# Attention's queries and keys kept channel by token, rotated from the bank by VectorE and GpSimd

## The chip, the cores and the metric

The kernel runs on 1 core of a Trainium2 chip. The metric is the device time of one execution in microseconds (us), the lower the better. The engines are TensorE (PE in the profile, its weight loads PEld), VectorE (DVE), ScalarE (ACT), GpSimd (POOL) and SyncE (SP), which here only starts DMAs. Each runs its own instructions in order, and they meet through semaphores.

## The reference, cut to what matters

One layer, 512 tokens, width 1024, all in float32. The normed input is multiplied by one wide matrix whose columns are split into sixteen parts; two branches follow (a sparse attention that takes the 128 best keys by an index score, and an mLSTM), then a gated merge.

```python
h = rmsnorm(x, norm_g[l])
(a_q, a_k, a_v, a_z, i_q, i_k, i_w,
 b_q, b_k, b_v, b_z, b_o, b_i, b_f, g_a, g_b) = jnp.split(h @ w_in[l], offsets, axis=-1)
q_a = partial_rope(a_q.reshape(Bsz, S, A_HEADS, A_HEAD_DIM), pos)   # 8 heads of 64
k_a = partial_rope(a_k.reshape(Bsz, S, A_HEADS, A_HEAD_DIM), pos)

def partial_rope(x, pos):            # of each 64 channels the first 16 turn
    ...
    x1, x2, rest = x32[..., :half], x32[..., half:rd], x32[..., rd:]
    out = jnp.concatenate([x1 * cos - x2 * sin, x1 * sin + x2 * cos, rest], axis=-1)
```

The attention's logits need `q_a` and `k_a` with channels on the partitions, the other way round than a product with tokens on the partitions leaves them.

## The kernel before

**Units and quarters.** A product of float32 numbers is made as three matmuls of rounded parts: `w_hi` and `w_lo` are a weight and its remainder, `h_hi` and `h_lo` those of the normed input (`three`, lines 1486 to 1488). The input projection is cut into units, each one PSUM bank `pj` of 128 by 512, made of 24 matmuls. `GROUPS` orders them: `iq0`, `iq1`, `aq`, `ak`, `bq`, `bk`, `bv`, `av`, `bo`, `bz`, `az`; a group is four units (three for the two `iq`). Units are written `bq0` to `bq3` below. In `aq` and `ak` a unit is one tile of 128 tokens, all 512 channels (token by channel). In `CHAN_GROUPS` (`bq`, `bk`) a unit is 128 channels, all 512 tokens.

A unit has four quarters, and `plan()` hangs every other job on a quarter, by number: `ak` is quarters 44 to 59, `bq` 60 to 75, `bk` 76 to 91, `bv` 92 to 107, `av` begins at 108. All engines walk the same table in the same order, so the table sets what is queued behind what. At a unit's last quarter ScalarE first empties the bank (`evacuate`, which also feeds VectorE), then does that quarter's side jobs, then rounds weights (`round_slot`, line 875), then the silu of the unit before (line 1043). GpSimd makes each weight's remainder (`remainder`, line 529). VectorE's own work of a unit (`unit(u)`) comes behind all side jobs of its quarters.

**What unit u + 2 waits for.** There are two `pj` banks, so TensorE may start a unit only when the unit two before has been read (`wait_unit_read`):

```python
elif UNITS[u] in STAGED:
    eng.wait_ge(rotated, STAGED.index(UNITS[u]) + 1)
elif UNITS[u][0] in CHAN_GROUPS:
    eng.wait_ge(conv_done, u - UNIT[("bq", 0)] + 1)
```

For `bq` and `bk` that is `conv(b)` on VectorE: three multiply-adds of about 510 elements from the bank (line 1234), after ScalarE's start of it (`conv_acc`, line 1000).

**Queries and keys of the attention before.** A unit of `aq` or `ak` is copied by ScalarE into `stage` (line 992); VectorE turns the 16 rotated channels of each head from the bank (three operations, lines 1138, 1140, 1141); TensorE turns the tile over with four transposes into a bank `tr` (line 1541); ScalarE copies it into `q_a` (line 904), or for keys rounds it into `k_parts` (line 913, two halves of 64 partitions), and VectorE writes the remainders, again from the bank (line 1259, two). This `stage_chan` job stands six quarters behind the unit's first.

**VectorE's other work here.** `round_plan` hangs the rounds of the top-k search on quarters: a round is a maximum (line 1223) and a replacement (line 1224). From quarter 73 on two rounds, of the second and of the first score tile, stand together every three quarters.

Of the kernel before, what the change touches and what calls it, by code (L numbers as in the profile page):

```python
# [19 lines left out]
ALU = mybir.AluOpType  # L20
# [18 lines left out]
ROT = A_DIM // 4  # L39
HALF = ROT // 2  # L40
# [20 lines left out]
CHAN_GROUPS = ("bq", "bk")  # L61

# [4 lines left out]
STAGED = [u for u in UNITS if u[0] in ("iq0", "iq1", "aq", "ak")]  # L67
# [44 lines left out]
def plan():  # L112
# [10 lines left out]
    put(first["iq0"] + 8, "gate_rows", 1)  # L123
    put(first["iq0"] + 8, "gate_rows", 0)
    put(first["iq1"] + 3, "gate_cols")
    for n, u in enumerate(STAGED):
        put(4 * UNIT[u] + 4 + 2, "stage_chan", n)

# [42 lines left out]
NOT_PE = ("scales_in", "scales", "decay_b")  # L171
# [52 lines left out]
def hybrid_kernel(nc, x, norm_g, w_in, conv_w, conv_b, b_igate, b_fgate, head_norm_g,  # L224
                  w_branch_a, w_branch_b, w_out, final_norm_g, ident_d, rope_d, out):
    ctx = ExitStack()
    with ctx:
# [58 lines left out]
        gate_l = const("gate_l", [P, TILES, 2 * B_HEADS])  # L286
# [45 lines left out]
        a_row = at("a_row", [B_HEADS, SEQ], F32, z_c + 8192)  # L332
        nm_row = at("nm_row", [B_HEADS, SEQ], F32, z_c + 10240)
# [207 lines left out]
        def wait_read(eng, job):  # L541
# [36 lines left out]
        def wait_unit_read(eng, u):  # L578
# [33 lines left out]
        def part(job, e):  # L612
# [4 lines left out]
            if g == "ak":  # L617
                cols = slice(j * P, (j + 1) * P)
                return src, k_parts[same, e, :, cols], k_parts[other, e, :, cols]
# [4 lines left out]
        def part_unit(job):  # L624

            return job[1] if job[1] < N_IQ else job[1] - TILES
# [22 lines left out]
        def _(sp):  # L649
# [36 lines left out]
            for n in range(LATE0):  # L686
# [48 lines left out]
        def _(pool):  # L735
# [13 lines left out]
            pool.memset(mask0[0:CHUNK, CHUNK:P], MASKED).then_inc(pool_step, 1)  # L749

            def side(p):
# [17 lines left out]
                for job in SIDE.get(p, []):  # L769
                    if job[0] == "decay_b":  # L770
# [74 lines left out]
        def _(act):  # L845
# [41 lines left out]
            def job_side(job):  # L887
# [13 lines left out]
                elif kind == "stage_chan" and STAGED[job[1]][0] == "aq":  # L901
                    j = STAGED[job[1]][1]
                    wait_full(act, job)
                    act.activation(q_a[:, j, :, :],
                                   bank_of(job)[:, :].rearrange("p (b t) -> p b t", t=P), ACT.Copy)\
                        .then_inc(q_a_turned, 1)
                elif kind == "stage_chan":
                    if STAGED[job[1]] == ("ak", 0):
                        act.wait_ge(gate_tok_made, 1)
# [46 lines left out]
                elif kind == "pv_b":  # L956
                    h, g = job[1:]
                    wait_full(act, job)
                    act.activation(cell[:, 2 * g:2 * g + 2, h, :],
# [20 lines left out]
            def evacuate(u):  # L980
# [6 lines left out]
                elif g in ("iq0", "iq1", "aq", "ak"):  # L987
# [18 lines left out]
                elif g == "av":  # L1006
                    act.activation(v_a[:, j, :], src[:, :], ACT.Copy).then_inc(done, 1)
# [8 lines left out]
            def split_queries(i):  # L1016
# [5 lines left out]
                act.wait_ge(q_a_turned, i + 1)  # L1022
# [88 lines left out]
        def _(dve):  # L1111
# [40 lines left out]

            def small(job):
# [597 lines left out]
```

## Time and profile before

| what | value |
|---|---|
| median of 3 runs | 505.25 us (505.06 to 505.51) |
| the profiled execution | 505.35 us, of which the span of its instructions 503.6 us |
| mean granted TensorE clock | 0.998 |
| TensorE busy | 494.5 us, 98% of the span |
| VectorE, ScalarE, GpSimd busy | 261.4, 239.2 and 213.0 us |

An engine's busy time is the union of its instructions. TensorE's matmuls overlap one another, so the pace of a stretch is read from the distance of starts, not from a row's duration. The averages hide stages: VectorE is busy in 52% of the span, but in 40 equal slices its digits read 9, 9, 9 from about 138 to 176 us, which is the stage of `bq`, `bk` and the first of `bv`.

### The profile page before, as it was taken

To read this page: it belongs to the slowest core of one execution; us is meant where nothing else is said; L and a number is where in the kernel's file an instruction comes from. 1 tells how busy PE (TensorE), PEld (TensorE's weight loads), DVE (VectorE), ACT (ScalarE), POOL (GpSimd) and SP (SyncE) were. 2 spreads that over 40 slices of the span, in tenths; PEclk is the share of its full clock that TensorE was granted. 3 is DMA by queue.
4 is the path that set the end of the run, shared out by engine and by line. 5 is a ranking of instruction groups with operands and counts; after the bars stand their busy time and mean duration, and the time that the engine had idled before them with its cause. 6 is when DMAs were issued, how large, how long until landed. Compare 5 with 4: busy or idle time off the path is not lost.

```text
span 503.6 us, 6823 instructions
## 1 busy us (share of the span) xinstructions
PE 494.5 (98%) x2518; PEld 411.6 (82%) x2518; DVE 261.4 (52%) x575; ACT 239.2 (47%) x434; POOL 213.0 (42%) x130
## 2 busy tenths in 40 slices
PE   8999999999999999999999999999999999999995
PEld 7688888888888888888788888888888888887885
DVE  3865777877899936525655567531111011125433
ACT  6757655555554455536568652413330333152322
POOL 0675131333344444247487451246534663373000
PEclk9999999999999999999999999999999999999999
DMA  8654432212343243112223112043234426453111
GB/s 284 188 153 128 126 87 79 84 48 80 83 111 99 85 117 104 52 43 85 57 70 85 43 43 65 20 125 104 62 87 125 126 58 193 126 149 144 42 55 72
DMA packets 44841, 48.94 MB, mean 97 GB/s; under 512 B 4996, under 2 KB 30212, under 8 KB 44808
## 3 DMA queue, kind: packets, MB, share of 16 engines
q1 hardware_dynamic: 43944, 47.65, 32.3%
q10 hardware_dynamic: 864, 0.86, 0.5%
q8 instruction: 20, 0.33, 0.3%
q14 instruction: 13, 0.11, 0.1%
HBM read 46.40 MB, written 2.11 MB: 96 GB/s over the span
## 4 chain that ended last, share of the span: by engine, by line
PE 94%; DMA 2%; SPq 1%; POOL 1%; ACT 1%; DVE 1%; issue 1%; DVEq 0%
PE pj L1486 24%; PE pj L1487 24%; PE pj L1488 24%; DMA w_raw<-in_w_in 2%; PE ob L1617 2%; PE tr L1606 2%; PE qb L1554 2%; PE qb L1553 2%; PE ob L1487 1%; PE qb L1487 1%; PE ob L1488 1%; PE qb L1488 1%; PE ob L1486 1%; PE qb L1486 1%; PE tr L1541 1%; PE qb L1601 1%
## 5 line engine op out<-in xcount | busy, mean ns | idle before, releaser
L529 POOL TENSOR_TENSOR w_lo<-w_raw,w_hi 128x1024 fp32r<-128x1024 f32 x70 | 168.9, 2424 | 156.3 <-ACT w_hi L875 156.0
L1486 PE MATMUL pj<-w_hi,h_hi 128*128 128x512 f32 x272 | 109.6, 403 | 0.0
L1488 PE MATMUL pj<-w_hi,h_lo 128*128 128x512 f32 x272 | 106.5, 392 | 0.0
L1487 PE MATMUL pj<-w_lo,h_hi 128*128 128x512 f32 x272 | 106.4, 391 | 0.0
L1486 PE MATMUL pj<-h_hi,w_hi 128*128 128x512 f32 (+1 forms) x200 | 78.1, 390 | 1.0 <-DVE h_lo L1129 1.0
L875 ACT ACTIVATE w_hi<-w_raw 128x1024 fp32r<-128x1024 f32 (+1 forms) x72 | 73.5, 1045 | 9.8 <-DMA w_raw<-in_w_out 6.3
L1488 PE MATMUL pj<-h_hi,w_lo 128*128 128x512 f32 (+1 forms) x200 | 77.9, 389 | 0.0
L1487 PE MATMUL pj<-h_lo,w_hi 128*128 128x512 f32 (+1 forms) x200 | 77.8, 389 | 0.0
L1488 PEld LDWEIGHTS pj<-w_hi,h_lo 128*128 128x128 f32 x272 | 51.1, 188 | 11.4
L1486 PEld LDWEIGHTS pj<-w_hi,h_hi 128*128 128x128 f32 x272 | 51.2, 188 | 8.3 <-issue 0.2
L1487 PEld LDWEIGHTS pj<-w_lo,h_hi 128*128 128x128 f32 x272 | 51.3, 188 | 8.0
L1443 DVE TENSOR_TENSOR prod<-qb,sig 128x512 f32<-128x512 f32 x8 | 5.5, 690 | 77.2 <-PE qb L1488 77.2
L1486 PEld LDWEIGHTS pj<-h_hi,w_hi 128*128 128x128 f32 (+1 forms) x200 | 37.3, 186 | 9.4 <-issue 1.3
L1488 PEld LDWEIGHTS pj<-h_hi,w_lo 128*128 128x128 f32 (+1 forms) x200 | 37.3, 186 | 8.1
L1487 PEld LDWEIGHTS pj<-h_lo,w_hi 128*128 128x128 f32 (+1 forms) x200 | 37.3, 186 | 7.8
L840 POOL TENSOR_TENSOR m_lo<-prod,m_hi 128x512 fp32r<-128x512 f32 x8 | 10.6, 1330 | 60.5 <-ACT m_hi L1088 60.5
L1211 DVE SCALAR_TENSOR_TENSOR score<-ob,idx_w,score 128x512 f32<-128x512 f32 (+2 forms) x45 | 27.7, 616 | 11.5 <-ACT ob L921 8.8
L921 ACT ACTIVATE ob<-qb 128x512 f32<-128x512 f32 (+2 forms) x48 | 22.0, 476 | 16.7 <-PE qb L1554 11.7
L966 ACT ACTIVATE probs<-probs,neg_max 128x128 f32<-128x128 f32 (+3 forms) x32 | 18.0, 562 | 23.3 <-DVE neg_max L1306 23.1
L1088 ACT ACTIVATE m_hi<-prod 128x512 fp32r<-128x512 f32 x8 | 5.1, 632 | 47.3 <-DVE prod L1446 47.3
L1315 DVE COPY probs_t<-tr 128x128 f32<-128x128 f32 (+3 forms) x32 | 15.6, 489 | 22.6 <-PE tr L1606 22.6
L1223 DVE MAX8 top<-score 128x8 f32<-128x512 f32 (+2 forms) x48 | 26.7, 556 | 0.9
(216 smaller groups left out, 817.3 us busy)
## 6 DMA issues: line engine op xcount, KB each, us to landing
w_raw<-in_w_in SPq DMA_DIRECT2D x60, 512.0 KB, 3.6
w_raw<-in_w_out SPq DMA_DIRECT2D x5, 512.0 KB, 3.5
x_tok<-in_x SPq DMA_DIRECT2D x4, 512.0 KB, 5.3
w_raw<-in_w_branch_a SPq DMA_DIRECT2D x8, 256.0 KB, 2.9
w_raw<-in_w_branch_b SPq DMA_DIRECT2D x8, 256.0 KB, 3.3
x_again<-in_x SPq DMA_DIRECT2D x1, 2048.0 KB, 9.3
w_late<-in_w_out SPq DMA_DIRECT2D x3, 512.0 KB, 6.1
out<-y_norm SPq DMA_DIRECT2D x4, 320.0 KB, 2.3
```

Source lines behind the costliest of these rows:

```text
L529: eng.tensor_tensor(lo[:, 0:m], raw_slot(n)[:, 0:m], hi[:, 0:m].bitcast(F32), ALU.subtract).then_inc(lo_by_dve if n in DVE_SLOTS else lo_b ...
L840: pool.tensor_tensor(m_lo[:, c, :], prod[:, c % 2, 0, :], m_hi[:, c, :].bitcast(F32), ALU.subtract)\
L875: act.activation(split_slot(n)[0][:, 0:m], raw_slot(n)[:, 0:m], ACT.Copy).then_inc(hi_made, 1)
L921: act.activation(ob[s % RELUS][:, 0:w], bank_of(job)[:, 0:w], ACT.Relu, scale=float(IDX_DIM) ** -0.5).then_inc(relu_made, 1)
L966: act.activation(probs[:, s % 2, 0:w], probs[:, s % 2, 0:w], ACT.Exp, scale=-1.0, bias=neg_max[:, s:s + 1], accum_out=p_sum[:, s:s + 1])\
L1211: ins = dve.scalar_tensor_tensor(out=acc, in0=ob[s % RELUS][:, 0:w], scalar=wt, in1=acc, op0=ALU.mult, op1=ALU.add)
L1223: link(dve.max(top8[:, i, :], acc))
L1315: dve.tensor_copy(probs_t[:, s % QUAD, 0:w], bank_of(job)[:, 0:w]).then_inc(probs_t_made, 1)
L1486: pe.matmul(bank, a_hi, b_hi, start=first, stop=False)
L1487: pe.matmul(bank, a_hi, b_lo, start=False, stop=False)
L1488: return pe.matmul(bank, a_lo, b_hi, start=False, stop=last)
L1553: pe.matmul(bank[:, 0:w], queries, ik_hi[:, 0:w], start=True, stop=False)
```

## The change

Units of `aq` and `ak` become channel by token: the weight is the stationary operand, and the bank holds 128 channels (two heads) by 512 tokens. ScalarE keeps the raw bank in `raw_chan`; VectorE multiplies the whole bank by a cosine table `cos_t` (ones where nothing turns) into `q_a` or `k_chan`. Four DMAs a group, started by ScalarE (`swap`), fetch the partner channels into `swapped`; GpSimd multiplies them by `sin_t` and adds them (`turn`, two operations for each of eight units). The `stage_chan` jobs of the two groups, with their transposes, go. For keys a new job `parts` follows each turn: ScalarE copies the turned keys into a `tr` bank and rounds them into `k_parts`, and VectorE writes the two remainders from that bank. The tables `cos_t` and `sin_t` come out of the transpose that the gates already had: `gate_rows` is now one job of four 128 by 128 transposes (was eight of 4 rows), `gate_cols` four (was eight); four ScalarE copies spread the tables, and five GpSimd memsets at the start blank the tiles.

```diff
+TURNED = ("aq", "ak")
+TURNS = [(g, b) for g in TURNED for b in range(KW)]
-STAGED = [u for u in UNITS if u[0] in ("iq0", "iq1", "aq", "ak")]
+STAGED = [u for u in UNITS if u[0] in ("iq0", "iq1")]
...
+    for k in range(4):
+        put(first["ak"] + k, "swap", k)
+        put(first["ak"] + 9 + 3 * 6 + k, "swap", KW + k)
+    for m in range(len(TURNS)):
+        p = first["ak"] + 6 + 6 * m
+        put(p, "turn", m)
+        if TURNS[m][0] == "ak":
+            put(p + 4, "parts", m - KW)
...
+                    if job[0] == "turn":
+                        m = job[1]
+                        g, b = TURNS[m]
+                        pool.wait_ge(rope_made, 4)
+                        pool.wait_ge(swap_in, 64 * (TURNED.index(g) + 1))
+                        pool.tensor_tensor(swapped[:, b, :], swapped[:, b, :], sin_t[:, :], ALU.mult).then_inc(sin_made, 1)
+                        pool.wait_ge(sin_made, m + 1)
+                        pool.wait_ge(cos_made, m + 1)
+                        part = swapped[:, b, :].rearrange("p (t n) -> p t n", n=P)
+                        pool.tensor_tensor(turned_rows(g, b), turned_rows(g, b), part, ALU.add).then_inc(turned, 1)
...
+                elif kind == "swap":
+
+                    n, k = divmod(job[1], 4)
+                    act.wait_ge(unit_out, UNIT[(TURNED[n], KW - 1)] + 1)
+                    if n:
+                        act.wait_ge(turned, KW * n)
+                    e, half = divmod(k, 2)
+                    to, src = A_DIM * e + HALF * half, A_DIM * e + HALF * (1 - half)
+                    act.dma_start(swapped[to:to + HALF, :, :], raw_chan[n][src:src + HALF, :, :]).then_inc(swap_in, 16)
+                elif kind == "parts":
+                    b = job[1]
+                    if b == 0:
+                        act.wait_ge(gate_tok_made, 1)
+                    act.wait_ge(turned, KW + b + 1)
...
+                    act.activation(tr[b % 2][:, :], k_chan[:, b, :], ACT.Copy).then_inc(k_in_bank, 1)
+                    for e in range(2):
+                        _, src, hi, _ = k_part(b, e)
+                        act.activation(hi, src, ACT.Copy).then_inc(k_hi_made, 1)
...
+                elif kind == "parts":
+                    b = job[1]
+                    for e in range(2):
+                        src, _, hi, lo = k_part(b, e)
+                        dve.wait_ge(k_in_bank, b + 1)
+                        dve.wait_ge(k_hi_made, 2 * b + e + 1)
+                        dve.tensor_tensor(lo, src, hi.bitcast(F32), ALU.subtract).then_inc(k_lo_made, 1)
...
+                if g in TURNED:
+                    if g == "ak" and j == 0:
+                        dve.wait_ge(swap_in, 64)
+                    if (g, j) == ("aq", 0):
+                        dve.wait_ge(rope_made, 4)
+                    dve.wait_ge(unit_out, u + 1)
+                    dve.tensor_tensor(turned_rows(g, j), pj[u % 2][:, :].rearrange("p (t n) -> p t n", n=P),
+                                      cos_t[:, :].rearrange("p (t n) -> p t n", n=P), ALU.mult).then_inc(cos_made, 1)
...
-                        if g in CHAN_GROUPS:
+                        if g in CHAN_GROUPS + TURNED:
```

So the swaps of the keys hang on quarters 71 to 74, turns 2 to 7 on 62, 68, 74, 80, 86 and 92, and parts 0 to 3 on 78, 84, 90 and 96.

VectorE, before: the end of `bq3` (the convolution, line 1234) and what stands between it and the convolution of `bk0`. `score` and `top` are the top-k search's.

```order
L1234 SCALAR_TENSOR_TENSOR conv_acc<-pj,conv_w_col,conv_acc 128x511
L1223 MAX top_72<-score 128x8
L1224 MATCH_REPLACE score<-top_72,score 128x384
L1223 MAX top_72<-score 128x8
L1224 MATCH_REPLACE score<-top_72,score 128x256
L1223 MAX top_72<-score 128x8
L1224 MATCH_REPLACE score<-top_72,score 128x384
L1223 MAX top_72<-score 128x8
L1224 MATCH_REPLACE score<-top_72,score 128x256
L1234 SCALAR_TENSOR_TENSOR conv_acc<-pj,conv_w_col,conv_acc 128x509
```

The same place in the change (the convolution is line 1305 there, the rounds 1294 and 1295):

```order
L1305 SCALAR_TENSOR_TENSOR conv_acc<-pj,conv_w_col,conv_acc 128x511
L1294 MAX top_71<-score 128x8
L1295 MATCH_REPLACE score<-top_71,score 128x384
L1294 MAX top_71<-score 128x8
L1295 MATCH_REPLACE score<-top_71,score 128x256
L1332 TENSOR_TENSOR k_parts<-tr,k_parts 64x512 x2
L1294 MAX top_71<-score 128x8
L1295 MATCH_REPLACE score<-top_71,score 128x384
L1294 MAX top_71<-score 128x8
L1295 MATCH_REPLACE score<-top_71,score 128x256
L1305 SCALAR_TENSOR_TENSOR conv_acc<-pj,conv_w_col,conv_acc 128x509
```

The pair of key remainders now stands inside the stage of `bk`, here before the convolution of `bk0`, and again before those of `bk2` and `bk3` and in `bv`; before, the four pairs stood in `ak` and in `bq0`.

ScalarE in the change, from the silu of `bq0` (`qk_b`, with its table load, behind the bank of `bq1`) to the bank of `bk0`:

```order
L1115 ACTIVATE qk_b<-conv_acc 128x512
L918 ACTIVATE w_hi<-w_raw 128x1024
L1070 ACTIVATE conv_acc<-pj,conv_b_col,conv_w_col 128x512
L960 DMA swapped<-k_raw 8x2048
L1115 ACTIVATE qk_b<-conv_acc 128x512
L960 DMA swapped<-k_raw 8x2048 x2
L918 ACTIVATE w_hi<-w_raw 128x1024
L960 DMA swapped<-k_raw 8x2048
L1070 ACTIVATE conv_acc<-pj,conv_b_col,conv_w_col 128x512
L1115 ACTIVATE qk_b<-conv_acc 128x512
L918 ACTIVATE w_hi<-w_raw 128x1024
L971 ACTIVATE tr<-k_chan 128x512
```

Before, the same stretch had no DMA start and no copy to a `tr` bank: bank, silu, weight followed each other. GpSimd in the change, around turns 3 and 4:

```order
L554 TENSOR_TENSOR w_lo<-w_raw,w_hi 128x1024 x2
L808 TENSOR_TENSOR swapped<-swapped,sin_t 128x512
L812 TENSOR_TENSOR q_a<-q_a,swapped 128x4x128
L554 TENSOR_TENSOR w_lo<-w_raw,w_hi 128x1024
L808 TENSOR_TENSOR swapped<-swapped,sin_t 128x512
L812 TENSOR_TENSOR k_chan<-k_chan,swapped 128x512
L554 TENSOR_TENSOR w_lo<-w_raw,w_hi 128x1024 x2
```

Each pair is one turn, between the weight remainders that were GpSimd's only work here.

## Rows read from the trace of the kernel before

**Rows 1.** The page: busy us, share, instructions; then the ending chain by engine.

```profile
...
PE 494.5 (98%) x2518; PEld 411.6 (82%) x2518; DVE 261.4 (52%) x575; ACT 239.2 (47%) x434; POOL 213.0 (42%) x130
...
PE 94%; DMA 2%; SPq 1%; POOL 1%; ACT 1%; DVE 1%; issue 1%; DVEq 0%
```

**Rows 2.** Waits of TensorE, whole run: us in total, times, longest.

```profile
...
PE pj L1500 <- POOL score L749: 1.3, 1, 1.3
```

**Rows 3.** The chain that ended last: start us, us, what.

```profile
...
33.25 0.87 PE tr L1529 x8
...
44.60 0.58 PE tr L1535 x8
...
125.66 0.44 PE tr L1541 x4
```

**Rows 4.** Timeline of TensorE, 154 to 171 us: start us, us, instruction.

```profile
...
154.54 0.39 PE L1486 MATMUL pj<-h_hi,w_hi 128*128 128x512 f32 x1
...
165.42 0.39 PE L1486 MATMUL pj<-w_hi,h_hi 128*128 128x512 f32 x1
...
170.86 0.39 PE L1486 MATMUL pj<-w_hi,h_hi 128*128 128x512 f32 x1
```

**Rows 5.** Groups of instructions by line and form: busy us, mean ns, idle before.

```profile
...
L1541 PE MATMUL tr<-ident,stage 128*128 128x128 f32 x56 | 8.4, 271 | 0.0
...
L1345 DVE TENSOR_TENSOR oa_lo<-o_at,oa_hi 128x512 fp32r<-128x512 f32 x4 | 8.1, 2037 | 0.8 <-ACT oa_hi L973 0.8
...
L1500 PE MATMUL pj<-score 128*128 128x128 f32 x26 | 5.9, 425 | 1.3 <-POOL score L749 1.3
...
L1259 DVE TENSOR_TENSOR k_parts<-tr,k_parts 64x512 fp32r<-64x512 f32 x8 | 5.5, 689 | 2.9 <-ACT k_parts L913 2.7
...
L828 POOL TENSOR_TENSOR gated<-gated,norm_b_row 128x512 f32<-128x512 f32 x4 | 5.2, 1289 | 7.7 <-DVE gated L1387 7.6
...
L913 ACT ACTIVATE k_parts<-tr 64x512 fp32r<-64x512 f32 x8 | 4.7, 593 | 6.5 <-PE tr L1541 6.4
...
L1138 DVE TENSOR_TENSOR pj<-pj,rope 128x128 f32<-128x128 f32 x14 | 4.1, 294 | 0.2
```

**Rows 6.** Window: us, then PE, PEld, DVE, ACT, POOL busy.

```profile
...
144.00:166.00 22.00, 22.00 (x99) 18.22 (x98) 20.69 (x47) 9.34 (x13) 9.60 (x4) 1.00 0.34 96
```

**Rows 7.** Timeline of VectorE: start us, us, instruction, idle before.

```profile
...
126.82 1.41 DVE L1259 TENSOR_TENSOR k_parts<-tr,k_parts 64x512 fp32r<-64x512 f32 x2 [2.17 <-ACT k_parts L913]
...
129.78 2.32 DVE L1234 SCALAR_TENSOR_TENSOR conv_acc<-pj,conv_w_col,conv_acc 128x509 f32<-128x509 f32 x3
...
145.22 2.31 DVE L1234 SCALAR_TENSOR_TENSOR conv_acc<-pj,conv_w_col,conv_acc 128x509 f32<-128x509 f32 x3
147.46 0.55 DVE L1223 MAX8 top<-score 128x8 f32<-128x384 f32 x1
...
149.68 0.56 DVE L1223 MAX8 top<-score 128x8 f32<-128x384 f32 x1
...
151.92 2.31 DVE L1234 SCALAR_TENSOR_TENSOR conv_acc<-pj,conv_w_col,conv_acc 128x509 f32<-128x509 f32 x3
...
167.76 2.32 DVE L1234 SCALAR_TENSOR_TENSOR conv_acc<-pj,conv_w_col,conv_acc 128x509 f32<-128x509 f32 x3
```

**Rows 8.** Timeline of GpSimd, 136 us.

```profile
...
136.74 2.40 POOL L529 TENSOR_TENSOR w_lo<-w_raw,w_hi 128x1024 fp32r<-128x1024 f32 x1 [5.00 <-ACT w_hi L875]
```

**Rows 9.** Timeline of ScalarE, 133 to 139 us.

```profile
...
133.78 1.28 ACT L1043 ACT_TABLE_LOAD   x1
...
138.42 0.78 ACT L1000 ACTIVATE conv_acc<-pj,conv_b_col,conv_w_col 128x512 f32<-128x512 f32 x1 [1.76 <-PE pj L1488]
```

**Rows 10.** Timeline of ScalarE with its queue, start of the run.

```profile
...
0.81 0.40 ACTq L853 DMA_DIRECT2D ident<-const_ident  x1
```

**Rows 11.** DMA issues: tensors, queue, count, KB each, median us to landing.

```profile
...
out<-y_norm ACTq DMA_DIRECT2D x4, 192.0 KB, 2.6
...
ident<-const_ident ACTq DMA_DIRECT2D x1, 64.0 KB, 4.0
```

More of the change, by code:

```diff
@@ L39 @@
 ROT = A_DIM // 4
+ROWS = 64
 HALF = ROT // 2
@@ L122, in plan @@
     put(first["iq0"] + 3, "ik_chan")
-    put(first["iq0"] + 8, "gate_rows", 1)
-    put(first["iq0"] + 8, "gate_rows", 0)
+    put(first["iq0"] + 8, "gate_rows")
     put(first["iq1"] + 3, "gate_cols")
@@ L170 @@
            "score": "q", "qk_b": "q", "qk_a": "q", "pv_b": "o", "pv_a": "o", "kt_b": "tr", "state_b": "o"}
-NOT_PE = ("scales_in", "scales", "decay_b")
+NOT_PE = ("scales_in", "scales", "decay_b", "swap", "turn", "parts")
 def fills():
@@ L622, in part, with k_part, turned_rows @@
             return src, iq_parts[same, e, b0:b0 + 4, cols], iq_parts[other, e, b0:b0 + 4, cols]
-        def part_unit(job):
-            return job[1] if job[1] < N_IQ else job[1] - TILES
+        def k_part(b, e):
+            same, other = slice(e * A_DIM, (e + 1) * A_DIM), slice((1 - e) * A_DIM, (2 - e) * A_DIM)
+            return tr[b % 2][same, :], k_chan[same, b, :], k_parts[same, e, b, :], k_parts[other, e, b, :]
+        def turned_rows(g, b):
+            return (q_a[:, :, b, :] if g == "aq" else k_chan[:, b, :].rearrange("p (t n) -> p t n", n=P))
         def unit_slots(u):
@@ L706, in _ @@
                     sp.wait_ge(neg_m_kept, 16)
+                    wait_full(sp, ("gate_cols",))
                     for h in range(B_HEADS):
@@ L749, in _ @@
             pool.memset(mask0[0:CHUNK, CHUNK:P], MASKED).then_inc(pool_step, 1)
+            pool.memset(gate_l[:, :, :], 0.0)
+            pool.memset(two_rows[:, :], 0.0)
+            pool.memset(cos_t[:, :], 1.0)
+            pool.memset(sin_t[:, :], 0.0)
+            pool.memset(swapped[:, :, :], 0.0).then_inc(blank_made, 1)
             def side(p):
@@ L900, in job_side @@
                     act.activation(en_m[:, :, :], gate_tok[:, 1, :, :], ACT.Exp).then_inc(en_made, 1)
-                elif kind == "stage_chan" and STAGED[job[1]][0] == "aq":
-                    j = STAGED[job[1]][1]
+                elif kind == "gate_rows":
+                    act.wait_ge(blank_made, 1)
                     wait_full(act, job)
-                    act.activation(q_a[:, j, :, :],
-                                   bank_of(job)[:, :].rearrange("p (b t) -> p b t", t=P), ACT.Copy)\
-                        .then_inc(q_a_turned, 1)
+                    for first, dst in ((64, cos_t), (96, sin_t)):
+                        for rows in (slice(0, ROT), slice(A_DIM, A_DIM + ROT)):
+                            act.activation(dst[rows, :], bank_of(job)[first:first + ROT, :], ACT.Copy)\
+                                .then_inc(rope_made, 1)
+                elif kind == "swap":
[11 more added lines that the diff above has]
+                    act.wait_ge(turned, KW + b + 1)
+                    if b < 2:
+                        act.wait_ge(part_lo_made, 2 * len(STAGED))
+                        act.wait_ge(gate_tok_made, 1)
+                    else:
+                        act.wait_ge(k_lo_made, 2 * (b - 1))
+                    act.activation(tr[b % 2][:, :], k_chan[:, b, :], ACT.Copy).then_inc(k_in_bank, 1)
+                    for e in range(2):
+                        _, src, hi, _ = k_part(b, e)
+                        act.activation(hi, src, ACT.Copy).then_inc(k_hi_made, 1)
                 elif kind == "stage_chan":
-                    if STAGED[job[1]] == ("ak", 0):
-                        act.wait_ge(gate_tok_made, 1)
                     wait_full(act, job)
```

96 lines of the change are left out of this document (55 added, 41 removed).

## The prediction

> **What bounds the kernel now.** I read the page first: TensorE is busy 98% of the span and holds 94% of the chain that ended last [rows 1]. The waits of TensorE say that it is hardly ever kept: the longest wait of the run, 1.3 us, lies at the very start [rows 2]. So a matmul or transpose that goes is worth its own time on the chain, and anything else is worth nothing until it makes TensorE wait. The reader should therefore look for two things: what leaves TensorE, and how far each engine that TensorE could wait for is from being late.
>
> **What leaves TensorE.** In the chain a set of four transposes of `stage` takes 0.44 us [rows 3]. Eight sets go: 8 x 0.44 = 3.5 us. The eight transposes of `gate_rows` take 0.87 and become four full ones, 0.44: 0.4 us. `gate_cols` takes 0.58 for eight and becomes four, of a size between: 0.2 us, bounds 0 and 0.3. The 24 matmuls of a unit only change which operand is stationary. That costs nothing: bk2 and bk3 (channel by token) take 165.42 - 154.54 = 10.88, 5.44 each, and bv0 (token by channel) takes 170.86 - 165.42 = 5.44 [rows 4]. Together 4.15 us less, bounds 3.9 and 4.3.
>
> **What it costs the others, early.** GpSimd's five memsets lie where it waits for the first weights. VectorE's multiply of a bank by `cos_t` is one operation of 512 elements in place of three short ones, near 0.69 us (`k_parts`, 512 elements from a bank) against three like the 0.29 of line 1138 [rows 5], both behind the same ScalarE copy: nothing. The swaps of the queries start at quarter 44, six quarters before turn 0, with 1.4 us of matmuls a quarter: hidden. GpSimd gets 16 operations, but in `aq` to `bv` it only feeds weights that TensorE needs several quarters later. I cost all this at nothing; if one of them isn't hidden it is a wait of some tenths.
>
> **The stage that has no room.** Between 144 and 166 us VectorE is busy 20.69 of 22 us, while TensorE is busy all 22 [rows 6]. TensorE may start unit u + 2 when VectorE's convolution of u is done, so I put each convolution beside its deadline. Let 0 be the end of bq0: bk2 starts five units later, so 0 is 154.54 - 5 x 5.44 = 127.3 in this trace. The convolution of bk0 runs from 151.92 for 2.24 (the next instruction's start, as with bq3's: 147.46 - 145.22) [rows 7]: it ends at 154.16, and bk2 starts at 154.54. The room is 0.4 us. The one of bq0 ends at 132.0, deadline 132.8; the one of bk3 ends at 170.0, deadline 170.86. From bq0's convolution to bk3's, 40.2 us, VectorE hardly rests.
>
> The change takes four pairs of key remainders (1.41 us a pair) out of the time before bq0's convolution, where VectorE had idle time (2.17 before the last pair), and puts three into this stage. What it gains by that is small: VectorE can't run ahead of the bank, so the convolution of bq0 starts at 1.0 (0.2 until ScalarE starts, 0.8 to empty the bank) instead of 2.5.
>
> **The walk, with 0 at the end of bq0.** GpSimd finishes the weight remainder that stands ahead of turn 3 at 139.14, or 11.8 [rows 8]; that one is late because ScalarE loads a table (1.28 us) before its silu [rows 9]. A turn is two operations of 1.29 us, by the nearest, `gated<-gated,norm_b_row` [rows 5]: turn 3 ends at 14.4. ScalarE has emptied bq2 at 11.9 (138.42 + 0.78 = 139.2 [rows 9]) and now stands before the first key swap until 14.5, because `swapped` is still being read. Behind it wait a silu, a weight rounding and the bank of bq3. Starting a DMA holds ScalarE's queue for 0.40 [rows 10]. So: start 14.9, silu 15.5, two starts 16.3, rounding 17.3, start 17.7; the bank of bq3, full at 16.3, is emptied at 18.4, and its convolution runs 18.6 to 20.8 (before: 17.9 to 20.2). Two pairs of top-k rounds, 149.68 - 147.46 = 2.2 us [rows 7], bring VectorE to the key remainders at 23.0.
>
> The four swaps are SBUF to SBUF, 64 KB each from 8 partitions, a form that the trace lacks. The nearest rows take 2.6 us (192 KB, same queue) and 4.0 (64 KB, at the start, beside the input loads) [rows 11]. I take 2.6, since in this stage the queues are lightly loaded: landed at 20.3, turn 4 done at 23.0. Then ScalarE copies to the bank and rounds two halves, 0.59 each [rows 5]: ready at 24.3 and 24.9. VectorE has waited 1.3 us; remainders done at 25.8, two pairs of rounds at 28.0, convolution of bk0 at 30.3. bk2 could have started at 27.2: **TensorE waits 3.1 us**.
>
> From the end of that convolution to the end of bk3's, VectorE has three convolutions and four double rounds (7 x 2.23 = 15.6) and now two pairs of remainders (2 x 1.41 = 2.8): 18.4. TensorE has three units, 16.3. By then turns and roundings are ready ahead of VectorE. **TensorE waits 2.1 us more**, before bv1. The fourth pair falls in `bv`, where TensorE doesn't wait for VectorE; it is done some 10 us before `kt_b` asks for it.
>
> Sum, against the profiled execution's own 505.35 (0.1 above the median): 505.35 - 4.15 + 3.1 + 2.1 = **506.4 us**.
>
> **Bounds of the unknown prices.** The second wait depends on VectorE's work alone: 2.1; if the distances that I add up are off by 0.5 together, 1.6 to 2.6. The first depends on the chain turn 3, swap, turn 4, rounding. If the halves are ready when VectorE comes (no cost for a start, an instant landing) it is 0.6. With starts at 0.40 and a landing of 4.0 it is 4.5. If the starts held nothing and the landing took 2.6, it would be 1.7. Total of both 2.2 to 7.1: 503.4 to 508.3.
>
> On the price of a remainder the trace has two rows, far apart: 689 ns for each of the keys', read from a bank, and 2037 ns for `oa_lo`, 512 elements too but with both inputs in SBUF [rows 5]. The new ones read the bank, so I take 0.69. The Trainium skill, "SBUF — State Buffer", section "SBUF: two separate sides", says that GpSimd and a VectorE operation with two SBUF inputs lock a shared port pair against each other. By that rule the new turns on GpSimd slow neither the banked remainders nor the convolutions, and the sum stays; were the remainders unprotected, three pairs at up to 1.3 us more for each half would add 8 us of VectorE's time to this stage.
>
> **Rivals.**
> *Faster (12%).* VectorE absorbs the pairs: from 501.2 (no wait at all) to 504.2 (the first wait 0.9 or less). For it: VectorE is busy only 52% of the span [rows 1]. Against it: the room of 0.4 us before bk2. It decides if the halves are rounded when VectorE comes to them at 23.0; one microsecond later the gain is below 0.2%.
> *No change (16%).* Both waits come, the first only 0.9 to 2.1 us, because starting a DMA holds ScalarE less than the row says or turn 3 ends earlier: 504.2 to 505.4.
> *Two full waits, the forecast (62%).* 505.4 to 508.3, with about two thirds of it (40%) above 506.3.
> *Slower by the clock (6%).* A wait of 3 us is longer than any in this trace. The 26 warm-up matmuls after TensorE's first idle take 5.9 us, 0.225 each [rows 5], where transposes of the same shape take 0.11 [rows 3]. If such a stretch followed the first wait it would cost half of 5.9, 2.9 more: 509.3. The Trainium skill, "TensorE: Matmul & The Clock Gate", Part 1 (the HAM clock gate), says that the throttled clock is the default and activity releases it; by this rule a long enough wait has such a price, and the waits of this trace, up to 1.3 us, can't tell.
> *Slower by a weight (4%).* ScalarE's stall also delays the rounding of bk's last weight slot. It ends at 17.3, GpSimd's remainder 2.4 later [rows 8], 19.8; TensorE wants it three quarters into bk0, 16.3 + 4.1 = 20.4. If a DMA start held ScalarE 0.7 us instead of 0.4, TensorE would wait there too, some 0.5, and 507.5 would come of it all.
>
> **How the numbers follow.** A measurement of this kernel can tell about 0.2%, 1.0 us, from no change: below 504.2 is faster, above 506.3 slower. Faster 0.12; slower 0.40 + 0.06 + 0.04 = 0.50; same 0.16 + 0.22 = 0.38. The forecast is the likeliest case's sum, 506.4; its own range is 505.4 to 508.3. For 8 in 10 I leave out most of the faster case and of the clock's: 503.8 to 508.4.
>
> **What will show it.** Waits of TensorE on VectorE's `conv_acc`, one of about 3 us at the start of bk2 and one of about 2 at bv1, none else above 0.5. ScalarE idle some 2.7 us before the first key swap, and its row of `conv_acc` for bq3 late. VectorE idle near 1.3 us before the first `k_parts`. Transposes of `stage` 24 instead of 56. The forecast is wrong if turn 3 is done before ScalarE asks for it, if the swaps land in under 2 us, or if VectorE's top-k rounds are found further ahead than by 1.5 us; it is wrong upward if the queries' stage, where I see nothing, makes TensorE wait.

## The result, and the profile after

The change makes the kernel a little slower, by 0.45%: 507.41 us median of 7 runs (506.83 to 508.4), against 505.15 of the kernel before, measured beside it (505.03 to 505.51); the ratio is 1.0045, 95% interval 1.0035 to 1.0054. The forecast, 506.4, is 1.0 too low and its range (503.8 to 508.4) holds the time. The seven executions are not alike: 506.8 to 507.1 (three), 507.4 and 507.6, 508.2 and 508.4. The profiled one, 508.22 us, is one of the two longest. One execution of all that follow, of `sbuf_remainders`, ran at a granted clock of 0.85 throughout and took 552.19 us; no figure below includes it.

The waits of TensorE (us in total, times, longest), where before the longest was 1.3 [rows 2]:

```profile
PE pj L1572 <- DVE conv_acc L1305: 3.6, 2, 3.0
```

TensorE in order of time (start us, us, instruction, idle before), at the starts of bk2 and bv1, which answer to [rows 4]:

```profile
149.93 0.39 PE L1573 MATMUL pj<-h_lo,w_hi 128*128 128x512 f32 x1
150.15 0.39 PE L1574 MATMUL pj<-h_hi,w_lo 128*128 128x512 f32 x1
153.56 0.80 PE L1572 MATMUL pj<-h_hi,w_hi 128*128 128x512 f32 x1 [3.02 <-DVE conv_acc L1305]
154.16 0.63 PE L1573 MATMUL pj<-h_lo,w_hi 128*128 128x512 f32 x1
154.58 0.63 PE L1574 MATMUL pj<-h_hi,w_lo 128*128 128x512 f32 x1
...
158.85 0.63 PE L1572 MATMUL pj<-h_hi,w_hi 128*128 128x512 f32 x1
159.28 0.51 PE L1573 MATMUL pj<-h_lo,w_hi 128*128 128x512 f32 x1
159.62 0.40 PE L1574 MATMUL pj<-h_hi,w_lo 128*128 128x512 f32 x1
...
161.91 0.39 PE L1572 MATMUL pj<-h_hi,w_hi 128*128 128x512 f32 x1
...
173.50 0.50 PE L1572 MATMUL pj<-w_hi,h_hi 128*128 128x512 f32 x1 [0.55 <-DVE conv_acc L1305]
```

Two things are to be seen. The first wait has the forecast length and place. Behind it a run of matmuls (154.16 to 159.28) stands 0.43 us apart, which for 512 columns is 1.2 GHz, before the distance falls back to the 0.23 of the other stretches, where the granted clock is 1.00 (2.4 GHz). bk2 takes 161.91 - 153.56 = 8.35 us, 2.9 more than the 5.44 of before. The second wait, forecast at 2.1, is only 0.55.

The windows (busy us of PE, PEld, DVE, ACT, POOL, then the granted clock), beside [rows 6], show the clock at 0.84 over the stage, and TensorE busy 18.98 of 22 us:

```profile
144.00:166.00 22.00, 18.98 (x72) 15.09 (x71) 18.34 (x40) 11.90 (x18) 15.49 (x10) 0.84 0.34 96
```

The engines that TensorE waited for: ScalarE with its queue, GpSimd, and VectorE, from the second turn's end to the convolution of bk0 (beside [rows 7], [rows 8] and [rows 9]).

```profile
134.12 0.78 ACT L1070 ACTIVATE conv_acc<-pj,conv_b_col,conv_w_col 128x512 f32<-128x512 f32 x1 [1.76 <-PE pj L1574]
137.60 0.66 ACTq L960 DMA_DIRECT2D swapped<-k_raw  x1
138.30 0.63 ACT L1115 ACTIVATE qk_b<-conv_acc 128x512 f32<-128x512 f32 x1 [3.40 <-POOL q_a L812]
138.39 1.36 ACTq L960 DMA_DIRECT2D swapped<-k_raw  x2
139.85 1.06 ACT L918 ACTIVATE w_hi<-w_raw 128x1024 fp32r<-128x1024 f32 x1 [0.91 <-issue]
139.93 0.63 ACTq L960 DMA_DIRECT2D swapped<-k_raw  x1
140.81 0.76 ACT L1070 ACTIVATE conv_acc<-pj,conv_b_col,conv_w_col 128x512 f32<-128x512 f32 x1
...
146.77 1.27 ACT L974 ACTIVATE k_parts<-k_chan 64x512 fp32r<-64x512 f32 x2
```

```profile
134.79 1.28 POOL L808 TENSOR_TENSOR swapped<-swapped,sin_t 128x512 f32<-128x512 f32 x1
136.15 1.36 POOL L812 TENSOR_TENSOR q_a<-q_a,swapped 128x512 f32<-128x512 f32 x1
140.99 2.41 POOL L554 TENSOR_TENSOR w_lo<-w_raw,w_hi 128x1024 fp32r<-128x1024 f32 x1 [3.48 <-ACT w_hi L918]
143.49 1.29 POOL L808 TENSOR_TENSOR swapped<-swapped,sin_t 128x512 f32<-128x512 f32 x1
144.85 1.30 POOL L812 TENSOR_TENSOR k_chan<-k_chan,swapped 128x512 f32<-128x512 f32 x1
```

```profile
134.82 1.54 DVE L1297 TENSOR_SCALAR score<-score 128x512 f32<-128x512 f32 x1
...
141.68 2.32 DVE L1305 SCALAR_TENSOR_TENSOR conv_acc<-pj,conv_w_col,conv_acc 128x509 f32<-128x509 f32 x3 [0.85 <-ACT conv_acc L1070]
...
147.52 1.41 DVE L1332 TENSOR_TENSOR k_parts<-tr,k_parts 64x512 fp32r<-64x512 f32 x2 [1.41 <-ACT k_parts L974]
...
151.19 2.32 DVE L1305 SCALAR_TENSOR_TENSOR conv_acc<-pj,conv_w_col,conv_acc 128x509 f32<-128x509 f32 x3
```

ScalarE is idle for 3.40 us: 2.7 until GpSimd's turn 3 is done (forecast 2.7) and 0.7 for the first start of a swap. The other starts follow, and the bank of bq3, full at about 139.3, is read only from 140.81. VectorE stands 1.41 us until the keys' halves are rounded. One operation of VectorE, at 134.82, takes 1.54 us beside a turn of GpSimd that began at 134.79; in `both_moves`, below, it takes 0.43 without one.

### The profile page after: what moved, and what is told of

The parts are those of the page before. It is cut to its first block, busy times and chain, and to the rows that moved or that the text cites. A ratio compares the mean times of both kernels' runs of the same rounds, so it can differ in the third digit from the quotient of the medians.

```text
span 506.4 us, 6779 instructions
## 1 busy us (share of the span) xinstructions
PE 493.4 (97%) x2478; PEld 409.3 (81%) x2478; DVE 261.5 (52%) x560; ACT 241.9 (48%) x438; POOL 237.3 (47%) x151
## 4 chain that ended last, share of the span: by engine, by line
PE 86%; DVE 4%; issue 3%; DMA 2%; POOL 2%; ACT 2%; SPq 1%; ACTq 0%; DVEq 0%; POOLq 0%
PE pj L1572 22%; PE pj L1574 21%; PE pj L1573 21%; DMA w_raw<-in_w_in 2%; PE ob L1701 2%; PE tr L1690 2%; PE qb L1637 2%; PE qb L1636 2%; PE ob L1573 1%; PE qb L1573 1%; PE ob L1574 1%; PE qb L1574 1%; PE ob L1572 1%; PE qb L1572 1%; DVE conv_acc L1305 1%
## 5 line engine op out<-in xcount | busy, mean ns | idle before, releaser
L1572 PE MATMUL pj<-h_hi,w_hi 128*128 128x512 f32 (+1 forms) x264 | 104.6, 396 | 4.1 <-DVE conv_acc L1305 3.0
L1573 PE MATMUL pj<-h_lo,w_hi 128*128 128x512 f32 (+1 forms) x264 | 104.1, 394 | 0.0
L1574 PE MATMUL pj<-h_hi,w_lo 128*128 128x512 f32 (+1 forms) x264 | 103.9, 394 | 0.0
L1572 PE MATMUL pj<-w_hi,h_hi 128*128 128x512 f32 x208 | 84.6, 407 | 0.5 <-DVE conv_acc L1305 0.5
L1574 PE MATMUL pj<-w_hi,h_lo 128*128 128x512 f32 x208 | 81.5, 392 | 0.0
L1573 PE MATMUL pj<-w_lo,h_hi 128*128 128x512 f32 x208 | 81.3, 391 | 0.0
L1572 PEld LDWEIGHTS pj<-h_hi,w_hi 128*128 128x128 f32 (+1 forms) x264 | 50.0, 189 | 14.9 <-DVE conv_acc L1305 3.4
L1574 PEld LDWEIGHTS pj<-h_hi,w_lo 128*128 128x128 f32 (+1 forms) x264 | 50.0, 189 | 11.1
L1573 PEld LDWEIGHTS pj<-h_lo,w_hi 128*128 128x128 f32 (+1 forms) x264 | 50.1, 190 | 9.7
L1574 PEld LDWEIGHTS pj<-w_hi,h_lo 128*128 128x128 f32 x208 | 39.0, 188 | 8.7
L1034 ACT ACTIVATE probs<-probs,neg_max 128x128 f32<-128x128 f32 (+3 forms) x32 | 18.0, 562 | 23.2 <-DVE neg_max L1384 23.1
```

Of the source, the lines that this page charges most:

```text
L1034: act.activation(probs[:, s % 2, 0:w], probs[:, s % 2, 0:w], ACT.Exp, scale=-1.0, bias=neg_max[:, s:s + 1], accum_out=p_sum[:, s:s + 1])\
L1572: pe.matmul(bank, a_hi, b_hi, start=first, stop=False)
L1573: pe.matmul(bank, a_hi, b_lo, start=False, stop=False)
L1574: return pe.matmul(bank, a_lo, b_hi, start=False, stop=last)
```

## The experiments

Each is compared with the kernel before, 505.11 to 505.28 us where measured beside them. A diff is against the changed kernel where nothing else is said.

### The two moves

`parts_late` hangs the four `parts` on quarters 96, 99, 102, 105:

```diff
-            put(p + 4, "parts", m - KW)
+            put(first["bv"] + 4 + 3 * (m - KW), "parts", m - KW)
```

> The changed kernel with its four jobs `parts` (copy to the bank, two halves, two remainders) moved from quarters 78, 84, 90, 96 to 96, 99, 102, 105, out of the stage of `bk`. Theory (the loss is what stands on VectorE and ScalarE ahead of the convolutions of `bk`, and the halved clock after the first wait is a consequence of that wait's length): the convolution of bq3 still starts at 18.6 us after the end of bq0 because ScalarE still stands before the key swap, then 4.5 us of rounds and 2.2 of the convolution bring bk0's end to 27.5 against a deadline of 27.2. TensorE waits 0.3 us, the granted clock stays 1.00 in this stage, there is no wait at bv1: 505.15 - 4.15 + 0.3 = 501.3 us. Rival (the clock fell for another reason than the wait, such as the change's new DMAs or shorter bursts of transposes): the half clock from bk2 on stays and costs its 2.9 us: 504.2. Second rival (the remainders only move their cost, to a wait in bv or av, where weights and the gate jobs stand): 503 to 505, with a wait of TensorE after bv1.

Measured 501.74 us (501.65 to 502.21), ratio 0.9933 (0.9919 to 0.9946). The waits of TensorE, and the window of the stage:

```profile
PE pj L1572 <- DVE conv_acc L1305: 0.2, 1, 0.2
```

```profile
144.00:166.00 22.00, 21.81 (x97) 17.70 (x96) 20.78 (x48) 9.10 (x12) 18.34 (x11) 1.00 0.41 120
```

ScalarE's stall and the new DMAs are still there, and the clock stays at 1.00: the first rival falls, and with no wait after bv1 the second too. The time is 0.4 above the expectation.

`turns_early` hangs the queries' turns on 50, 54, 58, 62 and leaves the rest:

```diff
-        p = first["ak"] + 6 + 6 * m
+        p = first["ak"] + 6 + (4 * m if m < KW else 6 * m)
```

> The changed kernel with the queries' turns at quarters 50, 54, 58, 62 in place of 50, 56, 62, 68; the key turns and `parts` stay. This takes ScalarE's idle time before the first key swap away, and leaves VectorE's extra pairs of remainders. Theory (first wait = late halves, a chain of turn 3, swap, turn 4, rounding; second = VectorE's load): ScalarE no longer waits 3.4 us, bq3's convolution starts near 18, the halves are ready when VectorE comes; remainders and rounds end at 26.0, bk0's convolution at 28.2: the first wait is about 1.0 us (0.6 to 1.6), the clock stays 1.00, and the second wait, at bv1, now shows at its full 2.1. Sum 505.15 - 4.15 + 1.0 + 2.1 = 504.1 us. Rival (VectorE's load alone makes the first wait): it stays near 3 us, the clock falls, and the time stays at 507.4. Rival on the clock (any new wait here halves it): 1.0 + 2.9 and a small second wait, about 505.4.

Measured 505.51 us (505.2 to 506.8, 11 runs), ratio 1.0008 (0.9999 to 1.0016), 1.4 above the expectation. The time alone would fit the rival on the clock (505.4); the trace rules that rival out, since the clock is 1.00 behind both waits. TensorE in order of time:

```profile
152.23 0.50 PE L1572 MATMUL pj<-h_hi,w_hi 128*128 128x512 f32 x1 [1.59 <-DVE conv_acc L1305]
153.04 0.40 PE L1572 MATMUL pj<-h_hi,w_hi 128*128 128x512 f32 x1
...
168.04 0.39 PE L1572 MATMUL pj<-w_hi,h_hi 128*128 128x512 f32 x1
170.85 0.50 PE L1572 MATMUL pj<-w_hi,h_hi 128*128 128x512 f32 x1 [1.97 <-DVE conv_acc L1305]
171.66 0.40 PE L1572 MATMUL pj<-w_hi,h_hi 128*128 128x512 f32 x1
```

The mechanism is as expected: the first wait about halves, the clock stays (it fell in one execution of the eleven, 506.8 at a mean clock of 0.993), and the second appears at its size. Two sizes are off. The first wait is 1.6, since GpSimd now waits for the landing of the swaps (ScalarE's queue, then GpSimd):

```profile
136.75 0.63 ACTq L960 DMA_DIRECT2D swapped<-k_raw  x1
```

```profile
137.81 2.41 POOL L554 TENSOR_TENSOR w_lo<-w_raw,w_hi 128x1024 fp32r<-128x1024 f32 x1 [2.75 <-ACT w_hi L918]
142.14 1.30 POOL L808 TENSOR_TENSOR swapped<-swapped,sin_t 128x512 f32<-128x512 f32 x1 [1.92 <-DMA swapped<-k_raw]
```

The last start was over at 136.75 + 0.63 = 137.38, so the landing took 4.8 us. And a wait costs 0.3 more than its row: in the trace above, from 168.04 to 171.66 there are two groups of three matmuls, 1.36, and 2.26 more, of which the row names 1.97. Of the 0.29, 0.16 is counting: the row begins at the end of the last matmul (0.39 long), while matmuls start 0.23 apart. The other 0.13 is the first group behind the wait, 0.81 long and not 0.68. With `both_moves` as the base the sum is 501.15 + 1.6 + 2.0 + 0.6 = 505.35, near enough.

`both_moves` has both edits.

> Both moves together: the queries' turns at quarters 50, 54, 58, 62 and `parts` at 96, 99, 102, 105. Theory: no wait of TensorE in bk or bv above 0.3 us, clock 1.00 throughout, 505.15 - 4.15 = 501.0 us, so 0.3 less than with `parts` moved alone. If it is equal to that one within 0.2 us, ScalarE's stall before the key swap costs nothing once the remainders are gone. If it is slower, the earlier turns are queued ahead of a weight remainder that TensorE wants in ak, and a wait on w_lo shows there.

Measured 501.15 us (501.1 to 501.91), ratio 0.9922 (0.9909 to 0.9936): the fastest version, 0.6 below `parts_late`, so the stall had a small price even there: the wait of 0.2 and the 0.3 that a wait costs beside its row make 0.5 of it. TensorE's window is full, as before the change, and the clock 1.00:

```profile
144.00:166.00 22.00, 22.00 (x99) 18.22 (x98) 20.25 (x48) 9.10 (x12) 17.37 (x11) 1.00 0.33 96
```

VectorE's operation of line 1297 meets no turn of GpSimd here:

```profile
134.81 0.43 DVE L1297 TENSOR_SCALAR score<-score 128x512 f32<-128x512 f32 x1
```

This is what the transposes were worth with nothing given back: 505.12 - 501.15 = 3.97 us.

### The wait and the clock

`before_max3`, `before_max5` and `before_max7` have none of the change; in the kernel before, VectorE repeats a maximum three, five or seven times ahead of the convolution of bk0:

```diff
+                for _ in range(7 if (i, r) == (2, 2) else 0):
+                    link(dve.max(top8[:, i, :], acc))
```

> The kernel before with three more maxima of the same tile ahead of the convolution of bk0: a wait of 3 x 0.57 - 0.4 = 1.3 us at bk2. Theory (a short wait costs itself and 0.3 for the refilled pipeline, and the clock stays, as in turns_early after 1.6): 505.2 + 1.6 = 506.8 us in every execution. Rival (the room on VectorE's side is larger than the 0.4 that I read): below 506.3.

> The kernel before with the maximum of one score tile written five times more, just ahead of the convolution of bk0 (it finds the same eight values again; nothing of the computation changes). TensorE then waits at bk2 for 5 x 0.57 less the room of 0.4, 2.45 us, between the 1.97 us after which the clock stayed and the 3.02 after which it fell. Theory (the clock falls with the length of the wait, wherever it comes from): either no fall, 505.12 + 2.45 + 0.3 (pipeline refilled) = 507.9, or a fall as after 3.02, with up to 3 more: 510.9. Rival (the fall belongs to something of the change): no fall here nor with seven.

> The same with seven maxima: a wait of 7 x 0.57 - 0.4 = 3.6 us in the kernel before, with none of the change in it. Theory (a wait of 3 us or more halves the clock for the next stretch, whatever made it): bk2 takes 8 us or more instead of 5.44, and the time is 505.12 + 3.6 + 0.3 + 2.9 = 511.9 us. Rival (the fall belongs to the change, its DMAs or its bursts): the clock stays 1.00 and the time is 505.12 + 3.9 = 509.0 us.

The waits came out at 1.4, 2.6 and 3.8 us. With three, all four executions lie at 506.75 to 506.95, as expected. With five, one took 508.06 at a mean clock of 0.998 and three 509.43 to 509.57 at 0.994 or 0.995, between the two times that I had named (507.9 and 510.9). With seven, three took 510.6 to 510.9 at 0.995 and one 511.95 at 0.992; I had expected 511.9 of all. So the clock falls without the change too, and its price comes in steps of 1.1 to 1.5 us: none, one or two. Executions of one and the same program get different steps. In the profiled one with seven maxima TensorE starts again at full pace, and only 1.3 us later does the distance of two matmuls go to 0.43, for some 3 us:

```profile
158.04 0.50 PE L1488 MATMUL pj<-h_hi,w_hi 128*128 128x512 f32 x1 [3.77 <-DVE conv_acc L1236]
158.38 0.39 PE L1489 MATMUL pj<-h_lo,w_hi 128*128 128x512 f32 x1
...
159.34 0.63 PE L1490 MATMUL pj<-h_hi,w_lo 128*128 128x512 f32 x1
159.76 0.63 PE L1488 MATMUL pj<-h_hi,w_hi 128*128 128x512 f32 x1
...
162.72 0.39 PE L1489 MATMUL pj<-h_lo,w_hi 128*128 128x512 f32 x1
```

`filled` puts 24 transposes that serve nothing on TensorE where it waited:

```diff
+                if (g, j) == ("bk", 2):
+                    for _ in range(24):
+                        pe.transpose(ob[1][:, 0:P], ident[:, :], ident[:, :])
```

> The changed kernel with 24 transposes of `ident` into a PSUM bank that nothing reads, on TensorE ahead of bk2, where it waited 3.02 us. At 0.11 us each they fill 2.6 us of that wait; they serve nothing, and the computation stays. Theory (the clock fell because TensorE stood still, and VectorE's second wait was hidden by the slow matmuls): the clock stays 1.00, bk2 takes 5.4 us instead of 8.4, and the second wait at bv1 comes back with 2.0 to 2.5 in place of 0.55. Time 507.41 - 2.9 + 1.7 = 506.2 us, the forecast made before the change ran. Rival (transposes don't keep the clock, or the clock falls for another reason): 507.4. Second rival (the second wait was never there): 504.5.

Measured 507.0 us (506.84 to 508.56), ratio 1.0039 (1.0027 to 1.0052): 0.8 above the expectation. It is 0.4 below the changed kernel, which is not clear of noise (that one's ratio is 1.0035 to 1.0054), so the filling alone can't be shown to save time here. Four of six executions lie at 506.84 to 507.02 with clocks of 0.997 and more. The profiled one is of the other two: bk2 goes at full pace, the second wait is back, and the clock falls behind that one (the waits, and the window from 170 to 175 us).

```profile
PE pj L1572 <- DVE conv_acc L1305: 2.3, 2, 2.0
```

```profile
170.00:175.00 5.00, 2.98 (x10) 2.34 (x10) 4.39 (x13) 3.54 (x6) 3.18 (x3) 0.84 0.37 107
```

So the second rival falls too: VectorE's second lateness is there, and in the changed kernel the slow matmuls stand in front of it. Two runs were made to see the clock's price with nothing to hide it. `first_pair` leaves the first `parts` at quarter 78 and hangs the others on 99, 102, 105; `first_pair_filled` adds the 24 transposes.

```diff
-            put(p + 4, "parts", m - KW)
+            put(p + 4 if m == KW else first["bv"] + 4 + 3 * (m - KW), "parts", m - KW)
```

> The changed kernel with the first `parts` where it was (quarter 78) and the other three at 99, 102, 105. Theory (the first wait comes from turn 3, swap, turn 4 and the first pair; the second, and only it, from the pairs after it): the first wait stays at 3.0 us, there is none at bv1, and so nothing hides what the slow clock costs. An execution in which it doesn't fall takes 501.15 + 3.0 + 0.3 = 504.5 us, one that loses 1.5 takes 506.0, one that loses 2.9 takes 507.4. Rival (the second wait comes from something else of the stage, such as ScalarE's late bank): a wait of 1 us or more at bv1 stays, and the time is 507 or more even without a fall of the clock.

> The same with the 24 transposes that nothing reads ahead of bk2, so that TensorE stands still for 0.3 us there and not 3.0. Theory: the clock stays 1.00, the place still costs 3.0 to 3.3 us, and there is no other wait: 504.2 to 504.5 us in every execution. Its distance to the kernel without the filling, 1.5 to 3 us, is the price of the clock when nothing hides it. Rival (filling changes nothing, as its median of 507.0 against 507.4 may look): the same time as without it, within 0.3.

The single executions, with the mean clock of each group:

```
first_pair         504.60 504.69 504.77 504.90 505.18   0.997, 0.998
                   505.87 506.07 506.17 506.24 506.38   0.994, 0.995
                   507.40 507.41                        0.992
first_pair_filled  504.39 to 504.94, eleven             0.997 to 1.000
```

The medians are 505.97 (ratio 1.0012, 1.0002 to 1.0023) and 504.69 (0.9992, 0.9983 to 1.0001). The single executions lie near the three levels expected (504.5, 506.0, 507.4), and the filled kernel has only the lowest, 0.2 above its expectation. The distance of the medians, 1.3, is a little under the 1.5 to 3 expected, because five of the twelve unfilled executions lose nothing. The profiled one of `first_pair`, of the middle level, has one wait, 3.0, none at bv1, and half the slow matmuls of the changed kernel behind it:

```profile
PE pj L1572 <- DVE conv_acc L1305: 3.0, 1, 3.0
```

In the filled kernel the place looks so:

```profile
150.19 2.78 PE L1716 MATMUL ob<-ident 128*128 128x128 f32 x24
153.25 0.50 PE L1572 MATMUL pj<-h_hi,w_hi 128*128 128x512 f32 x1 [0.28 <-DVE conv_acc L1305]
153.58 0.39 PE L1573 MATMUL pj<-h_lo,w_hi 128*128 128x512 f32 x1
```

### Remainders from SBUF

`sbuf_remainders` drops ScalarE's copy to the bank; VectorE subtracts from `k_chan` itself. `sbuf_rem2` is the same kernel again.

```diff
-            return tr[b % 2][same, :], k_chan[same, b, :], k_parts[same, e, b, :], k_parts[other, e, b, :]
+            return k_chan[same, b, :], k_chan[same, b, :], k_parts[same, e, b, :], k_parts[other, e, b, :]
...
-                    act.activation(tr[b % 2][:, :], k_chan[:, b, :], ACT.Copy).then_inc(k_in_bank, 1)
```

> The changed kernel without ScalarE's copy of the turned keys to a bank: VectorE's remainders read k_chan in SBUF, beside k_parts in SBUF. Nothing of the computation changes. Theory (an fp32 VectorE operation between SBUF tiles is held while GpSimd works, as line 1297 shows in the changed kernel's trace, 1.54 us where it took 0.43 before): the eight remainders take 1.0 to 2.0 us each instead of 0.69, 2 to 7 us more of VectorE's time in the stage that has no room, of which ScalarE gives 0.6 back for each pair; the first wait grows from 3.0 to 3.5 to 5, the second comes back with 1 to 3: 508.5 to 512 us. Rival (the copy buys nothing): the remainders take 0.7, the halves are ready 0.6 earlier, the first wait is 2.4 and the time 506.8 or, if the clock then doesn't fall, 504 to 506. The Trainium skill, "SBUF — State Buffer", section "SBUF: two separate sides", has the rule of the shared port; by it the first theory holds.

> The same kernel as sbuf_remainders, whose profile fell in an execution with a clock of 0.85 throughout, while its other executions gave 509.6 to 513.5. Expected: the remainders again near 1.18 us each on average, those under a GpSimd operation above 1.2 and the others near 0.7, a first wait of 3.5 to 5 us followed by half the clock, 509 to 513 us.

Three executions of `sbuf_remainders` gave 509.55, 511.09 and 513.49 (ratio 1.0121, 1.0092 to 1.0151), and `sbuf_rem2` 511.16 us median (510.99 to 513.66), ratio 1.0128 (1.011 to 1.0146); in its trace TensorE waits 3.8 and 2.1 us. The tile's row, and its pairs in order of time, of `sbuf_rem2`:

```profile
L1330 DVE TENSOR_TENSOR k_parts<-k_chan,k_parts x8: 685/1028/2094, 147.2 to 179.5; 64x512 fp32r<-64x512 f32 x8
```

```profile
147.18 2.81 DVE L1330 TENSOR_TENSOR k_parts<-k_chan,k_parts 64x512 fp32r<-64x512 f32 x2 [0.81 <-ACT k_parts L973]
...
159.07 3.07 DVE L1330 TENSOR_TENSOR k_parts<-k_chan,k_parts 64x512 fp32r<-64x512 f32 x2
...
168.87 1.41 DVE L1330 TENSOR_TENSOR k_parts<-k_chan,k_parts 64x512 fp32r<-64x512 f32 x2
```

GpSimd there:

```profile
146.32 2.41 POOL L554 TENSOR_TENSOR w_lo<-w_raw,w_hi 128x1024 fp32r<-128x1024 f32 x1
...
169.78 2.76 POOL L554 TENSOR_TENSOR w_lo<-w_raw,w_hi 128x1024 fp32r<-128x1024 f32 x1 [2.80 <-ACT w_hi L918]
```

The pairs that begin under a GpSimd operation take 2.81 us (two of them) and 3.07; the one that begins 0.9 ahead of one takes 1.41, and there GpSimd's operation is the longer, 2.76 in place of 2.41. From the bank all eight remainders take 0.68 to 0.69. So the copy, 0.6 us of ScalarE for each turn, pays: without it the kernel loses 3.8 us more (511.16 against 507.41). The Trainium skill, "SBUF — State Buffer", section "SBUF: two separate sides", has this as a lock of a shared port pair. The rows agree: GpSimd's operation ends at 148.73, 1.55 after the first pair began, and the pair takes 1.40 longer than from the bank.

## Why the prediction was right, and where it was not

**The gain** was 4.15 by the sum and 3.97 by `both_moves`; four sets a group went, `gate_rows` fell to 0.44 and `gate_cols` to 0.39. Right within its bounds.

**The first wait** was 3.1 and came at 3.02 by its row, 3.2 between starts, as the forecast counts. Counted from the end of bq0 (now 123.04), in us:

| step | forecast | trace after |
|---|---|---|
| turn 3 done | 14.4 | 14.5 |
| convolution of bq3 begins | 18.6 | 18.6 |
| turn 4 done | 23.0 | 23.1 |
| VectorE idle before the first pair | 1.3 | 1.41 |
| convolution of bk0 done | 30.3 | 30.5 |
| bk2 could have begun | 27.2 | 27.3 |

Two steps in it were wrong and did no harm. A DMA start held ScalarE's queue for 0.63 to 0.68, not 0.40, but the silu ran beside it. The landing was not what turn 4 waited for: GpSimd's weight remainder, behind ScalarE's stall, ended at 143.40, or 20.4, where the forecast had the landing at 20.3. That turn 4 came out right to 0.1 is luck in this step. With the stall gone the landing shows, 4.8 us, outside my 2.6 to 4.0. That I had not foreseen, and it makes 0.6 of the 1.4 by which `turns_early` missed its expectation.

**The second wait** was 2.1. VectorE's chain from bk0's convolution to bk3's was put at 18.4 and took 18.6 in `filled` (153.43 to 172.06), where the wait is 2.0 by its row. Right; `first_pair`, with the pairs gone from there, shows none.

**What the sum lacked** is the slow first group behind each wait, 0.13; the other 0.16 of the 0.3 was in it, since it counted starts. Its gain was 0.2 too large. By the rows, 505.15 - 3.97 + 3.0 + 2.0 + 0.6 = 506.8, and the executions of `filled` without a slow stretch take 506.9. So about half of the 1.0 by which the forecast was low is in such small terms, and half is the clock.

**The clock** is the step that failed. The forecast kept it at full speed behind a wait of 3 us, gave its fall 6% and put 2.9 on top of both waits, 509.3. By the mean clocks, 0.991 to 0.996 where the kernel before has 0.997 to 1.000, it fell in every execution of the changed kernel (one was profiled), and its 2.9 were not added: slow matmuls and VectorE's lateness lie side by side. Where TensorE loses 1.5, the second wait can shrink by as much: the three executions at a clock of 0.994 and 506.8 to 507.1 take no longer than those of `filled` that lose nothing (this is read from times, since no such execution was profiled). Where it loses 2.9, units and price are 16.3 + 2.9 = 19.2 against VectorE's 18.6, with bk2's bank late for VectorE in turn (idle 1.35 before 163.00), and the profiled execution took 19.9 from bk2 to bv1: 1.3 more than in `filled`. The median is 0.5 above the 506.9 of a kernel that keeps its clock; why that execution, 507.41 at 0.994, and the one of 507.63 at 0.996 lie between the levels no trace shows. With no second wait behind it, in `first_pair`, it costs its whole 1.5 or 2.8.

**The rivals.** "Faster" named the right condition, the halves ready at 23.0; the first was ready at 24.4, and it did not come. "Slower by a weight" had its condition nearly met (a start held 0.63 to 0.68), and missed by nothing: the remainder ended at 143.40, the matmul that needs it stood due at 143.44, and no wait on `w_lo` shows. What decides is where the four `parts` stand: moved by 9 to 18 quarters, the same change is 0.7 to 0.8% faster than before.

**What stays open:** why one execution loses 1.5 us of clock behind a wait and the next none or twice that; and why the keys' swaps need 4.8 us in `turns_early` and, turn 4 being no later than 143.49, at most 2.9 behind the last start in the changed kernel.

## What to carry to other kernels

When work leaves the bounding engine, look up for each stage which engine has the least room there, and put the new work where that engine has time to spare: the four `parts` cost 5.7 us in one stage (two waits and what the clock added) and almost nothing 9 to 18 quarters later. Two prices that fall on the same stretch, TensorE's slow clock and VectorE's lateness, were compared here and not added: the clock cost 1.3 of its 2.9 us with VectorE late behind it, and all of it without. In the same way the filler saved 1.3 us of the median without a second late engine, and with one nothing that is clear of noise. A wait of the bounding engine costs its length, some tenths to get going again, and possibly its clock: here never after 1.4 us, always after 3.8.

## What the runs showed of the hardware

- The clock behind a wait of TensorE, one execution told from another by its time and mean clock: after 1.4 us it held in 4 of 4 executions, after 1.6 and 2.0 (both in one kernel) in 10 of 11, after 0.3 and 2.0 (`filled`) in 4 of 6, after 2.6 in 1 of 4, after 3.0 in 5 of 12 (`first_pair`) and 0 of 7 (the changed kernel), after 3.8 in none of 4, and after 3.8 and 2.1 (`sbuf_rem2`) in none of 4. The slow stretch began at once behind the wait in the changed kernel and in `first_pair`, and 1.0 to 1.3 us later in `before_max7`, `filled` and `sbuf_rem2`. The clock came back by itself with TensorE at work (at 159.3 in the changed kernel), as the Trainium skill, "TensorE: Matmul & The Clock Gate", Part 1, has it (activity releases the throttled clock).
- 24 transposes of 128 by 128 that nothing reads held it in 11 of 11 executions when they stood in the same gap of 3.0 us (`first_pair_filled`).
- A 128x512 VectorE `TENSOR_SCALAR` between SBUF tiles took 1.54 us in the changed kernel, where it met a GpSimd operation just begun, and 0.43 in `both_moves` and in the kernel before.
- A DMA start on ScalarE's queue from 8 partitions held it for 0.63 to 0.68 us in the keys' swaps (1.24 in the first of the queries'), while one activation ran beside it.
